# Experts' results scattered to token rows and read back by plain loads, with a sixth weight slot

## The reference, cut to what matters

```
def _moe(h, router_w, router_bias, w_gate, w_up, w_down):
    ...                                   # sigmoid scores, best group of 4, top 2 experts inside it
    gates = jnp.sum(jax.nn.one_hot(idx, N_EXPERTS) * wsel[..., None], axis=1)
    a = jnp.einsum('td,edf->tef', x, w_gate)
    up = jnp.einsum('td,edf->tef', x, w_up)
    mid = jax.nn.silu(a) * up * gates[:, :, None]
    y = jnp.einsum('tef,efd->td', mid, w_down)
```

## Time and profile before

| | value |
|---|---|
| median of 3 runs | 951.83 us |
| profiled execution | 950.9 us |
| its span | 949.0 us |
| PE busy | 799.0 us (84%) |
| DVE / ACT / POOL busy | 378.7 / 270.8 / 96.6 us |
| mean granted TensorE clock | 0.927 |
| DMA moved | 226.45 MB |
| of it on the software queue (POOL) | 21.62 MB |
| of it on ACT's queue | 10.25 MB |
| layer 0 experts, from first token transpose to last overflow result | 367.9 to 500.6 us |
| layer 1 experts, same | 780.0 to 921.9 us |

### The profile page before, as it was taken

The page is one execution under the profiler, slowest core; times in us unless marked ns, Lnnn a source line. Parts: engine busy times, 40 slices in busy tenths (PEclk is TensorE's granted clock), DMA queues, the critical chain, the costliest instruction groups (busy, mean ns, idle before and its releaser), DMA issues.

```text
span 949.0 us, 11487 instructions
## 1 busy us (share of the span) xinstructions
PE 799.0 (84%) x4035; PEld 440.2 (46%) x4035; DVE 378.7 (40%) x844; ACT 270.8 (29%) x631; POOL 96.6 (10%) x146
## 2 busy tenths in 40 slices
PE   4779999999888997999771779879899989998760
PEld 0237665635443455555430446545554665554330
DVE  3366582355154342422113444664642433321214
ACT  1241111310541242222112326555530431221211
POOL 2300000001000013000004002211200030000102
PEclk9989999999989997999996879999999959999985
DMA  9991154369970277999996936202118479999965
GB/s 278 367 339 52 46 146 160 113 203 349 273 314 0 89 254 249 374 413 409 410 382 224 370 113 246 91 1 90 47 41 315 152 250 336 403 410 412 393 233 199
DMA packets 85055, 226.45 MB, mean 239 GB/s; under 512 B 8596, under 2 KB 18509, under 8 KB 84681
## 3 DMA queue, kind: packets, MB, share of 16 engines
q1 hardware_dynamic: 72706, 193.89, 56.4%
q0 software_dynamic: 8576, 21.62, 7.1%
q10 hardware_dynamic: 3720, 10.25, 2.9%
HBM read 216.60 MB, written 17.78 MB: 247 GB/s over the span
## 4 chain that ended last, share of the span: by engine, by line
PE 62%; DMA 14%; DVE 9%; issue 7%; ACT 3%; SPq 3%; DVEq 2%; POOLq 0%; POOL 0%; ACTq 0%
PE ps L869 55%; DMA ring<-in_moe_w_up_dram 5%; PE ps L876 4%; DMA arena<-in_moe_w_up_dram 3%; DMA ring<-in_w_mod_dram 2%; PE ps L1096 2%; SPq L655 2%; DVEq L1842 2%; SPq L638 1%; DVE negmax L1895 1%; DMA arena<-y_rows,rows_out 1%; DMA hT<-h_rows,rows_in 1%; DVE xn L2286 1%; DMA mod_rows<-modrow 1%; ACT hT L1557 1%
## 5 line engine op out<-in xcount | busy, mean ns | idle before, releaser
L869 PE MATMUL ps<-arena 128*64 128x256 f32 (+13 forms) x1084 | 229.3, 453 | 28.5 <-DMA arena<-in_moe_w_down_dram 7.3
L869 PEld LDWEIGHTS ps<-arena 128*64 128x64 f32 (+4 forms) x1084 | 123.7, 172 | 117.7 <-issue 67.0
L869 PE MATMUL ps<-ring,hT 128*128 128x512 f32 (+2 forms) x384 | 133.6, 507 | 6.5 <-issue 5.9
L869 PE MATMUL ps<-ring,arena 128*64 128x256 f32 (+1 forms) x864 | 124.8, 432 | 10.7 <-DMA ring<-in_moe_w_up_dram 6.6
L869 PEld LDWEIGHTS ps<-ring,hT 128*128 128x128 f32 x384 | 73.0, 192 | 64.9 <-issue 60.5
L869 PEld LDWEIGHTS ps<-ring,arena 128*64 128x64 f32 x864 | 60.3, 136 | 60.5 <-issue 34.8
L876 PE MATMUL ps<-ident,arena 128*128 128x128 f32 (+2 forms) x332 | 51.5, 294 | 19.7 <-DVE hT L1901 4.6
L1514 ACT ACTIVATE arena<-ps 128x256 f32<-128x256 f32 (+5 forms) x88 | 38.7, 454 | 94.1 <-PE ps L869 87.5
L2226 DVE TENSOR_TENSOR arena<-arena,ps 128x128 f32<-128x128 f32 x37 | 10.6, 288 | 133.2 <-ACT arena L1619 133.2
L869 PE MATMUL ps<-hT,ring 128*128 128x384 f32 x192 | 62.1, 486 | 0.0
L869 PE MATMUL ps<-ring,condT 128*32 128x512 f32 x384 | 54.9, 699 | 8.4 <-DMA ring<-in_w_mod_dram 7.7
(11 more groups left out here) (295 smaller groups left out, 841.0 us busy)
## 6 DMA issues: line engine op xcount, KB each, us to landing
ring<-in_w_mod_dram SPq DMA_DIRECT2D x48, 1024.0 KB, 9.2
ring<-in_moe_w_down_dram SPq DMA_DIRECT2D x24, 1024.0 KB, 17.9
ring<-in_moe_w_gate_dram SPq DMA_DIRECT2D x42, 512.0 KB, 14.3
ring<-in_moe_w_up_dram SPq DMA_DIRECT2D x42, 512.0 KB, 16.4
arena<-in_moe_w_gate_dram SPq DMA_DIRECT2D x32, 512.0 KB, 8.2
arena<-in_moe_w_up_dram SPq DMA_DIRECT2D x32, 512.0 KB, 10.1
arena<-in_moe_w_down_dram SPq DMA_DIRECT2D x13, 1024.0 KB, 12.1
ring<-in_ev_w_in_dram SPq DMA_DIRECT2D x9, 1024.0 KB, 13.1
```

The source lines that it names most:

```text
L869: mm = pe.matmul(out, lhsT, rhs, **kw)
```

## The change

The results' DRAM buffer `y_rows` gets 2 x 384 rows: row t is the first choice of token t, row 384+t the second. The plan matmuls now give two lists instead of one: the token to gather (as before) and the row to scatter to. POOL writes each pair of results with an indirect DMA to those rows, and the bounds check drops empty places. In the overflow loop POOL does the same for each block, after its gather, instead of ACT's store. Pairs 0 to 6 count on `y_stored`, pair 7 is the first count of `over_stored`. The zero rows are gone. Reading back is six plain loads of 128 rows, three issued by ACT and three by SP. `NEARLY` becomes 6: a sixth early slot lies behind the fifth in `arena`, where `qkv` (layer 0) and moved modulation rows (layer 1) lay, with waits before its first fill; 18 pieces per layer go through early slots and 30 through the ring.

```diff
-NROWS = NMAIN + NOVER * HALF
-NEARLY, CYCLES = 5, 3
+NEARLY, CYCLES = 6, 3
...
-    c["ids"] = np.arange(T).reshape(NT, P).T - NO_ROW
+    token = np.arange(T).reshape(NT, P).T - NO_ROW
+    c["ids"] = np.concatenate([token, token, token, token + T], 1)
...
-        y_rows = nc.dram_tensor("y_rows", [NROWS, D], F32, kind="Internal").ap()
+        y_rows = nc.dram_tensor("y_rows", [2 * T, D], F32, kind="Internal").ap()
...
@@ SP, send_early and after send_over
                 for k, entry in enumerate(early[l]):
+                    if k == NEARLY - 1 and l == 0:
+                        sp.wait_ge(stored, 32)
+                        for t in range(NT):
+                            drained_wait(sp, "gO", t)
+                    if k == NEARLY - 1 and l == 1:
+                        last = MOVED.index(CHUNKS["mla"][-1])
+                        sp.wait_ge(mod_out[last % 2], 16 * (last // 2 + 1))
                     fill_early(k, entry)
...
+            def rows_back(l, nb):
+                sp.wait_ge(y_stored[0][l], 16 * (NPAIR // 2))
+                sp.wait_ge(y_stored[1][l], 16 * (NPAIR // 2 - 1))
+                sp.wait_ge(over_stored[l], nb * 16 + 16)
+                for t in range(NT):
+                    sp.dma_start(y_of[1][:, t, :], y_rows[T + P * t:T + P * t + P, :]).then_inc(y_back[t], 16)
...
@@ POOL
-            pool.dma_start(y_rows[NMAIN:NROWS, :], d["zero_row"].partition_broadcast(NROWS - NMAIN)).then_inc(rows_zeroed, 16)
...
+                def scatter(c):
+                    for half in range(2):
+                        pool.wait_ge(y_read[half][l], 2 * c + 2)
+                    pool.indirect_dma_start(y_rows, bass.IndirectOffsetOnAxis(ap=rows_in[:, NPAIR + c:NPAIR + c + 1], axis=0), ysb[:, c % 2, :], None,
+                                            bounds_check=2 * T - 1, oob_is_err=False).then_inc(over_stored[l] if c == NPAIR - 1 else y_stored[c % 2][l], 16)
+
+                for c in range(3):
+                    scatter(c)
                 pool.wait_ge(over_rows[l], 1)
...
+                for c in range(3, NPAIR):
+                    scatter(c)
                 nb = blocks_of(pool, l)
                 with pool.Fori(0, nb) as b:
                     pool.wait_ge(row_ready[l], b + 1)
...
                         over_gathered[l], 16)
                     pool.drain()
+                    pool.wait_ge(over_done[l], b + 2)
+                    pool.wait_ge(y_read[1][l], b + (NE + 1))
+                    pool.tensor_tensor(pool_mark[:, :], pool_mark[:, :], pool_mark[:, :], ALU.mult)
+                    pool.indirect_dma_start(y_rows, bass.IndirectOffsetOnAxis(ap=to_now[0:HALF, :], axis=0), ysb[0:HALF, 0, :], None,
+                                            bounds_check=2 * T - 1, oob_is_err=False).then_inc(over_stored[l], 16)
+                    pool.drain()
...
-                for t in range(NT):
-                    for s in range(2):
-                        pool.indirect_dma_start(y_of[s][:, t, :], None, y_rows, bass.IndirectOffsetOnAxis(ap=rows_out[:, 2 * t + s:2 * t + s + 1], axis=0)).then_inc(
-                            y_back[t], 16)
...
@@ PE, plan matmuls (16 and 22 columns for 8 and 11)
-                    mm = product(bank[:, 0:NPAIR], hit[:, i, :], pair_ids[:, 8 * i:8 * i + 8], start=i == 0, stop=i == 2 * NT - 1)
+                    mm = product(bank[:, 0:2 * NPAIR], hit[:, i, :], row_table[:, 2 * NPAIR * i:2 * NPAIR * i + 2 * NPAIR], start=i == 0, stop=i == 2 * NT - 1)
...
@@ ACT, experts
-                    if e % 2 and e >= 3:
-                        store((e - 3) // 2)
...
-                store(NPAIR - 1)
...
                     result(ysb[0:HALF, 0, 0:512], 0, over_done)
-                    act.wait_ge(over_done[l], b + 2)
-                    act.wait_ge(y_read[1][l], b + (NE + 1))
-                    act.dma_start(y_rows[bass.ds(b * HALF + NMAIN, HALF), :], ysb[0:HALF, 0, :]).then_inc(over_stored[l], 16)
+                act.wait_ge(y_stored[1][l], 16 * (NPAIR // 2 - 1))
+                act.wait_ge(over_stored[l], nb * 16 + 16)
+                for t in range(NT):
+                    act.dma_start(y_of[0][:, t, :], y_rows[P * t:P * t + P, :]).then_inc(y_back[t], 16)
...
@@ DVE, plan_rows, over_lists and the overflow loop
-                dve.tensor_tensor(tabs, tabs, ids[:, :].unsqueeze(1).unsqueeze(3).broadcast_to([P, 2, NT, NPAIR]), ALU.mult)
+                dve.tensor_tensor(row_table[:, 0:4 * NT * NPAIR].rearrange("p (i k c) -> p k i c", k=2, c=NPAIR), by(pair_ids, NPAIR).unsqueeze(1).broadcast_to([P, 2, 2 * NT, NPAIR]),
+                                  ids[:, :, :].unsqueeze(3).broadcast_to([P, 2, 2 * NT, NPAIR]), ALU.mult)
...
+                dve.tensor_scalar(rows_to[0:HALF, :], ps[MT_BANKS[0]][0:HALF, 256 + NOVER:256 + 2 * NOVER], float(NO_ROW), None, ALU.add)
...
+                    dve.tensor_copy(to_now[0:HALF, :], rows_to[0:HALF, bass.ds(b, 1)])
+                    settle()
                     result(ysb[0:HALF, 0, 512:], 0)
```

More of the change, by code:

```diff
@@ L397, in build_step @@
         cv = sb("cv", P, KVH * HD)
+        rows_to, to_now = ck[:, 0:NOVER].bitcast(mybir.dt.int32), ck[:, 16:17].bitcast(mybir.dt.int32)
+        ids = ck[:, 32:32 + 4 * NT].rearrange("p (k i) -> p k i", k=2)
         filtc = sb("filtc", HID, 3 + 2 * HID)
@@ L690, in send_over @@
                     sp.dma_start(early_w[:, OVER_SLOT[2], :].rearrange("p (j n) -> p j n", n=D), src).then_inc(over_full[2][l], 16)
+                return nb
+            def rows_back(l, nb):
[4 more added lines that the diff above has]
+                    sp.dma_start(y_of[1][:, t, :], y_rows[T + P * t:T + P * t + P, :]).then_inc(y_back[t], 16)
             for i, entry in enumerate(pieces):
@@ L696, in _ @@
                 if i == at["after0"]:
-                    send_over(0)
+                    nb = send_over(0)
                 if i == at["in1.1"] + 1:
+                    rows_back(0, nb)
                     for t in range(NT):
@@ L781, in _ @@
                 load(pool, in_route, slots, d["slots"])
-                load(pool, in_route, ids[:, :], d["ids"])
+                load(pool, in_route, ids[:, :, :], d["ids"].rearrange("p (k i) -> p k i", k=2))
                 for t in range(NT):
@@ L786, in _ @@
                     pool.dma_start(h_rows[l][P * t:P * t + P, :], htok[:, t, :]).then_inc(h_stored, 16)
-                pool.wait_ge(rows_zeroed, 16)
                 pool.wait_ge(h_stored, 16 * NT * (l + 1))
                 pool.drain()
-                pool.wait_ge(rows_ready[l], 1)
+                pool.wait_ge(rows_ready, l + 1)
                 for c in range(NPAIR):
@@ L810, in _ @@
                 pool.drain()
-                for c in range(2):
-                    pool.wait_ge(y_stored[c][l], 16 * (NPAIR // 2))
-                for t in range(NT):
-                    for s in range(2):
-                        pool.indirect_dma_start(y_of[s][:, t, :], None, y_rows, bass.IndirectOffsetOnAxis(ap=rows_out[:, 2 * t + s:2 * t + s + 1], axis=0)).then_inc(
-                            y_back[t], 16)
                 if l == 1:
@@ L1185, in experts @@
                         for i in range(2 * NT):
-                            mm = product(bank[0:HALF, 256:256 + NOVER], hit_over[:, i, :], place_block[:, 16 * i:16 * i + NOVER], start=i == 0, stop=i == 2 * NT - 1)
+                            mm = product(bank[0:HALF, 256:256 + 2 * NOVER], hit_over[:, i, :], row_table[:, 2 * NOVER * i:2 * NOVER * i + 2 * NOVER], start=i == 0, stop=i == 2 * NT - 1)
                         mm.then_inc(over_idx[l], 1)
@@ L1625, in result @@
                     act.activation(dst, ps[Y_BANKS[e % 2]][0:HALF, :], ACT.Copy).then_inc(done[l], 1)
-                def store(c):
-                    for half in range(2):
-                        act.wait_ge(y_read[half][l], 2 * c + 2)
-                    act.dma_start(y_rows[P * c:P * c + P, :], ysb[:, c % 2, :]).then_inc(y_stored[c % 2][l], 16)
                 def main_turned(e):
@@ L2100, in route @@
                 settle()
-                dve.tensor_tensor(both, masks[:, 0:48], masks[:, 48:96], ALU.add).then_inc(plan_sums[l], 1)
+                dve.tensor_tensor(both, masks[:, 0:48], masks[:, 48:96], ALU.add).then_inc(plan_sums, 1)
             def plan_rows(l):
```

35 lines of the change are left out of this document (15 added, 20 removed).

## The result

The changed kernel takes 977.75 us (median of 4 runs, 973.95 to 979.15), the kernel before 951.90 us on the same chip: a ratio of 1.0279 [1.0245, 1.0314]. The forecast was 971.0 us, the range 956 to 984. The profiled execution took 978.59 us at a mean granted clock of 0.889; before it was 950.9 us at 0.927. DMA moved 220.17 MB for 226.45. One run further down, of the last experiment, took 951.75 us in a slower state of the chip and is left out there.

What follows compares the result with a forecast made beforehand. The expert stage was taken to start bound by PE and end bound by the weight stream. Terms: 950.9 - 9.6 (stream) + 0.2 (plan) + 30.8 (loops) - 1.6 (reading back) = 970.7, stated as 971.0 us; range 956 to 984.

Steps and rivals of the forecast that it cites:

- The order on POOL: Overflow loops: gathers queue on POOL behind a late result, its scatter and a drain; both layers' loops together +30.8 us.
- the signs: Expected in the trace: drains over 4 us, next gather 6.5 us after a result, `turn_in` waiting, clock near one half.
- Rival A: Overflow loops: the drain behind a scatter does not hold POOL until landing; cycle 14 us, total 958.4; chance 0.16.
- The block-0 term: First overflow block of each layer: result 13.7 us after the last main result instead of 9.9; bounds 11.5 and 16.
- The cycle: Later overflow blocks, from one block's result to the next: 18.1 us; ends 15 and 21.
- The weight stream: Expert stage: sixth slot and smaller stores return 4.9 and 4.7 us of PE's late-weight waits, 9.6 us in all.
- the last expert: End of the main expert stage: the last expert loses about 1.2 us more to late weights, counted as recoverable.
- the slot: Sixth early slot, filled while DMA stands still: 1 MB less left to stream, 2.55 us a layer at 411 GB/s.
- the smaller stores: Result stores: at most 768 rows instead of 1024 per layer, some 2.4 us saved before the last weights land.
- The tail: Reading back after the last block's result: 10.1 us to the first tile instead of 11.0, counted as -0.8 a layer.
- transposes at 874: Sign in layer 1's expert stage: the transposes after expert 14 would start at 874 us, seen at 877.75 before.
- Zero rows, plan and main scatters at nothing: Removing zero rows: 0 us, at most 1 gained; plan: 0.1 us a layer; main scatters: 0 us, bounds 0 and 1.

Runs made afterwards that it cites:

- the last experiment: Changed kernel with block gathers sent ahead of the scatters, minus POOL's drain between the token rows' stores and first gathers: 942.10 us, 0.9890 of the kernel before.
- 60 filling transposes: Changed kernel with 60 useless identity transposes on PE in every overflow block, before the wait for gathered rows: 972.38 us, 1.0255 of the kernel before.
- gathers ahead and five slots: Changed kernel with each next block's gather sent ahead of the scatter, one drain fewer per iteration, and five early slots: 944.02 us, 0.9941 of the kernel before.
- its experiment: Changed kernel with the old write of 704 zero rows, to an unread buffer, and POOL's old wait put back: 981.96 us, 1.0310 of the kernel before.

## Why the prediction was right, and its sizes

**The order on POOL** was the step that carried the verdict, and the experiment that turned it shows that: 14.4 and 22.6 us of loop time went with the order, all scatters kept. Of the signs, `turn_in` waited for its gather in all five blocks, no indirect transfer came behind the last scatter, and the clock was near one half. The others held in part. The drains lasted 6.8 and 2.9 us in layer 0 and 5.8, 4.0 and 2.8 in layer 1, so not all over 4; the next gather left 8.6, 7.6 and 5.8 us after a result for 6.5.

**Rival A was half of a truth.** The drain does hold POOL until the scatter lands. In layer 1, where the landings are listed, it lasted 5.8 us for a landing of 5.5, 4.0 for 3.7 and 2.8 for 2.5, starting 0.2 us ahead of the issue. But A's price supposed that without it the gather would land as before. It lands late, in the weights that the same result calls for: without the drain behind the scatter it was 968.5 us and not 958.4.

**The block-0 term, 13.7 us forecast, was 16.9 and 16.5.** The gather came 2.5 and 2.3 us after the last main result (2.3 forecast) and landed in 6.7 and 6.8 us, not 6.0. PE then stood idle for 4.95 and 4.91 us where I had counted 3, and the granted clock was low for nearly the whole block: from transposes to result 7.65 and 7.3 us, and not 4.1 + 1.3. I took half of the clock's price for an idle time close to that which the earlier trace rows had shown to be enough. The two blocks 0 together came 6.0 us later than forecast. The 0.25 us that the prediction names for the added copy is also missing from this sum, and 0.2 + 1.0 + 1.0 is 2.2 and not 2.3; neither matters.

**The cycle, 18.1 us forecast, was 18.5, 18.4 and 15.6**, and that the first two came so near is luck: their terms offset each other. The scatter, with the drain to its end, took 6.5, 5.6 and 3.8 us (4.3 forecast), all three beside weights; only the last scatter of a layer was sent into silence, and landed in 2.5. The gather landed in 2.2, 3.1 and 2.1 us and not 4.9. From transposes to result the block took about 7.6 us and not 6.6 + 0.25, since the clock was low throughout. I had taken the gather's landing from a row with weight traffic around it, and the drain had moved it out of most of that traffic. Two of these three gathers move no rows at all. The row that I took, the gather at 487.53, is itself such an empty one, and it took 4.9 us beside weights.

The prediction set a rule of the Trainium skill (DMA: Bandwidth & Descriptors, Anatomy of one DMA) against its rows: about 2.0 us for a software-issued transfer plus its bytes at 436 GB/s. For a transfer of no rows that gives 2.0 us and for 0.09 MB 2.2, both estimates. The two empty gathers, at 2.2 and 2.1 us, and the last scatter of layer 1, 0.09 MB in 2.5 us, come near it when counted from the start of POOL's issue, so without the 1.0 us that the prediction added. The block-0 gathers' 6.7 and 6.8 us and the main scatters' 7.3, beside weights, do not. Nor was 4.8 us the best landing of an indirect transfer before, as the prediction has it: it is the best of L805 alone, and the first gather back (L815) landed in 4.2.

**The weight stream returned 7.1 us and not 9.6.** Up to the transposes behind expert 14 it gave all that the beat allows: in layer 0 they start 98.5 us after the first gather for 102.6, in layer 1 98.2 for 102.2, 4.1 us each (4.4 and 3.8 forecast). PE's timeline, to set against the earlier trace rows:

```profile
463.88 1.09 PE L1121 MATMUL ps<-ident,hT 128*128 128x128 f32 x8
...
886.49 1.09 PE L1121 MATMUL ps<-ident,hT 128*128 128x128 f32 x8
...
899.06 1.94 PE L894 MATMUL ps<-ring,arena 128*64 128x512 f32 x8 [1.37 <-DMA ring<-in_moe_w_down_dram]
```

The 1.2 us that I counted for the last expert did not come back (0.2 in layer 0), and in layer 1 another 1.2 were lost there, the last row's wait for down weights among them. Also the parts were sized wrongly: the slot gives 2.2 to 3.5 us a layer (2.55 forecast), the smaller stores 0.1 to 1.3 (2.4 forecast). Bytes saved in a stream that ends the same stage were not worth their time at 411 GB/s; why, no run tells.

**The tail gained 2.5 us a layer instead of 0.8.** First tile at ACT 8.4 us after the last result: 0.8 to the scatter's issue, 2.6 to land, 0.4 to issue the reads, 4.6 to ACT's first work. The scatter's landing was the term in error, again a quiet transfer priced by a loaded row. The chain of waits of the changed kernel (start, us, what):

```profile
513.83 2.56 DMA y_rows<-arena,ck
516.41 0.37 ACTq L1699
516.82 9.20 DMA xn<-y_rows
```

Its last row counts to a later tile, which the first join hides; ACT's first work on the rows starts at 521.46.

These errors offset each other too. Against the forecast, the profiled execution lost 6.0 us in the two blocks 0, 2.5 in the stream, 2.1 at the first gather and 2.8 between the layers; it won 3.5 in the tails and 1.9 in the cycles. That it ended within 8 us of the forecast is in part luck. The sign "transposes at 874" could not have come true even so: by the prediction's own terms layer 1 starts some 5.5 us later than before.

**Missed: layer 0's first gather, 2.2 us late.** The chain shows the store of the last token rows at 10.1 us, and a drain behind it; before, the slowest of the three stores took 6.0 us.

```profile
350.65 10.12 DMA h_rows<-xn
...
360.79 3.33 POOLq L804
```

A drain of 3.5 us stood behind the stores before, too. The slowest store took 9.6 to 10.4 us in eight of the nine profiled kernels with both the sixth slot and the scatters, but 6.6 in the ninth, that with 60 filling transposes. It took 6.4 us with the scatters and five slots, 6.7 with the slot alone and 8.3 with gathers ahead and five slots. Both parts together go with a late store, but neither that they are needed nor what slows it is shown.

**Zero rows, plan and main scatters at nothing**: the first is borne out by its experiment; for the others the stretches leave no room for more than a us, since the transposes behind expert 14 came by the beat.

## What to carry to other kernels

When a transfer is moved onto a queue that works in order, ask what is behind it there and who waits for that; a wait for a late result ahead of somebody's gather costs that result, the transfer and, with a drain, its landing. Put the request for the next step ahead of the store of this one: the same edits then gained 1.4% instead of losing 2.8%. Look also at the last turn of a loop, which may wait for a request that nobody needs; here it was PE's longest wait in layer 0's loop, and leaving it out was not tried. Before taking a wait away, look at what else the same event starts, since the freed transfer may only queue with it; and price a landing by a row with the same traffic around it.

## What the runs showed of the hardware

- A scatter of one block from SBUF to DRAM (64 rows of 4 KB in its list, places without a row left out) costs POOL 0.94 us and lands in 2.5 us in silence, 3.7 and 5.5 beside weights. A gather costs POOL 1.04 us. One that moves no rows lands in 2.1 and 2.2 us in silence, and took 4.9 beside weights in the kernel before (the one at 487.53); block 0's took 6.7 and 6.8 beside weights. POOL's queue moved 18.75 MB for 21.62, with the scatters added.
- A drain behind such a scatter lasts until the scatter has landed (5.8, 4.0 and 2.8 us for landings of 5.5, 3.7 and 2.5).
- 4.95 us of idle was followed by transposes and down matmuls all at the lower clock, 2.7 us more in the block; 2.03 us was followed by transposes at the full clock and down matmuls at the lower one, although PE had worked in between.
- Back to back at the full clock, 8, 24 and 60 transposes of 128x128 fp32 took 1.09, 2.84 and 6.77 us: 0.109 us for each further one and 0.22 once, whether they read the gathered tokens (the 8) or the identity.
